# A hybrid decoder layer with a mixture of experts on one core: down weights issued first on the DMA queue, row lists copied at the top of a block, activations turned at its end

## The chip, the cores and the metric

The kernel runs on one core of a Trainium2 chip. The metric is device time in microseconds (us) of one launch; the profile takes one execution and gives its span, which is a little shorter than the time.

## What is computed

One layer of a conditioned decoder for 1024 prompt tokens and 8 sample tokens, width 1024. A mixer part (adaLN, one wide input projection, a gated linear recurrence beside a short convolution, an output projection) is followed by a mixture of experts: 64 experts of width 256, 8 for each token. The experts' part, cut to what matters:

```python
def swiglu(x, w_gate, w_up, w_down):
    return (jax.nn.silu(x @ w_gate) * (x @ w_up)) @ w_down
# assignments sorted by expert, each expert's rows padded to blocks of 128 rows
def block(args):
    tok, e = args
    return swiglu(h_pad[tok], w_gate[e], w_up[e], w_down[e])
out = lax.map(block, (row_tok.reshape(n_blocks, MOE_BLOCK), blk_exp))
out = out.reshape(n_rows, D) * row_w[:, None]
return jax.ops.segment_sum(out, row_tok, num_segments=T + 1)[:T]
```

All inputs and outputs are f32. The change touches only this part.

## The kernel before, in words

The first 1090 us or so hold the mixer, the router and the sorting of rows. Then the function `experts` runs one body (`block_of(i, q)`) for each used block of 128 rows, 92 here, on every engine at once: a Fori over spans of 8 blocks, an If that skips an empty span, a Fori over two parts of 4 blocks, and 4 blocks unrolled, each under an If (`blocks`, L1937 to L1945). Each If loads a number from the tensor `table` into a register (`entry`, L1934), and further `entry` calls fetch a block's expert. These loads, branches and register operations are done by the engine's sequencer, which hands the arithmetic to the engine. Five engines share the work of a block:

- **POOL** gathers the 128 token rows of block i+4 (`gather`, L2050) and adds the result of block i to `acc_d` in HBM (L2070); each addition waits until the one before has landed.
- **PE** turns the gathered rows (`turn`, L2090, 8 transposes), multiplies by gate and up weights (`up`, L2099, 24 matmuls; each product is made of three with operands split into a rounded part `_hi` and a rest `_lo`), turns the gated activations `hh` (L2114, 2 transposes into bank 3) and multiplies by the down weights (6 matmuls at L2124 for the first half of the 256 rows, 4 at L2130, in f32, for the second). Its body for block i has the order: turn `hh` of block i, turn the rows of block i+2, `up` of block i+1, down of block i.
- **ACT** rounds: the turned rows (`take`, x_hi), the weights (`round_weights`, wexp_hi, two halves, and `round_down`, down_hi, between them), the turned activations (hTe is `h1`, L2183; hTe_hi is `h0_hi`, L2184). It also makes the silu (`gate`, sg, L2170), and the output rows `ob` scaled by the routing weight (L2192).
- **DVE** makes the rests: wexp_lo (L2214), down_lo (L2220), x_lo (L2204), hTe_lo (`turned`, L2224); the product sg times up (`gate`, L2228, which gives semaphore `h_ok`); and copies one column of `lists` for the gather (`to_gather`, L2231) and for the addition (`to_add`, L2234), and the routing weights (wcol, L2210), for which it waits for the gathered rows.
- **SP** issues the weight loads of an expert into one of four slots: gate and up, 2 MB in four transfers (`next_up`, L1882), once DVE has made the rests of the expert four before; down, 1 MB in two (`next_down`, L1895), once the down load before has landed and the expert four before has been used. Its loop takes, for expert n: gate and up of n, wait that those of n-1 have landed (`landed_up`), down of n-3.

Of the kernel before, what the change touches and what calls it, by code (L numbers as in the profile page):

```python
# [1898 lines left out]
def experts(nc, tidy, a, sb, sem, banks, ident, xe_d, acc_d, table, starts, total, lists, ix, xg, gat, wexp, wdn, up_in, down_in,  # L1899
# [3 lines left out]
    with ExitStack() as ctx:  # L1903
# [60 lines left out]
        with nc.Block() as block:  # L1964
            @block.sync
            def _(sp):
                def blocks_to(e):

                    return sp.value_load(starts[0:1, bass.ds(e, 1)], min_val=1, max_val=ITEMS)

                def landed_up(slot, round_):
                    sp.wait_ge(up_in[slot], 64 * round_ + 64)
                    sp.sem_inc(up_ok, 1)

                def next_up(part, g):

                    at, slot = part * EG + g, g % RING
                    sp.wait_ge(wlo_ok, blocks_to(at - 3) * 2)
                    load_up(sp, a, wexp, expert_at(part, g), slot, up_in[slot])

                def next_down(part, g):

                    at, slot = part * EG + g, g % RING
                    before = blocks_to(at - 3)
                    sp.wait_ge(down_in, 32 * at)
                    sp.wait_ge(dn_ps, before)
                    sp.wait_ge(dlo_ok, before)
                    load_down(sp, a, wdn, expert_at(part, g), slot, down_in)

                landed_up(0, 0)  # L1990
                landed_up(1, 0)
                for e in range(2, RING):
                    load_up(sp, a, wexp, expert_at(0, e), e, up_in[e])
                    sp.wait_ge(down_in, 32 * e)
                    load_down(sp, a, wdn, expert_at(0, e), e, down_in)
                for e in range(2, RING):
                    landed_up(e, 0)
                for j in range(RING, EG):
                    next_up(0, j)
                    if j > RING:  # L2000
                        landed_up(j - 1 - RING, 1)
                next_down(0, RING)
                with sp.Fori(1, GRP) as part:
                    for g in range(EG):
                        next_up(part, g)
                        if g in (0, RING):
                            landed_up(RING - 1, part * 2 - 1 + g // RING)
                        else:
                            landed_up((g - 1) % RING, part * 2 + g // RING)
                        next_down(part - (0 if g >= 3 else 1), (g - 3) % EG)  # L2010
                landed_up(RING - 1, E // RING - 1)
                for g in range(EG - 3, EG):
                    next_down(GRP - 1, g)
                for slot in range(2):
                    sp.wait_ge(wlo_ok, blocks_to(E - 3 + slot) * 2)
                    for t in range(4 * slot, 4 * slot + 4):
                        sp.dma_start(kept_tile(wexp, t), x2_d[t * P:(t + 1) * P, :]).then_inc(kept_in, 16)
                sp.wait_ge(wlo_ok, blocks_to(E - 1) * 2)
                sp.dma_start(kept_tile(wexp, TILES - 1)[0:NS, :], x2_d[T:, :]).then_inc(kept_in, 16)
                sp.dma_start(kept_tile(wexp, TILES), mod_d[NS:NS + 1, 5 * D:].to_broadcast([P, D])).then_inc(kept_in, 16)  # L2020
                sp.dma_start(kept_tile(wexp, TILES + 1)[0:NS, :], mod_d[0:NS, 5 * D:]).then_inc(kept_in, 16)
                sp.dma_start(kept_tile(wexp, TILES + 2), a["final_norm_g"].rearrange("(a n) -> a n", a=1).to_broadcast([P, D])
                             ).then_inc(kept_in, 16)
                sp.wait_ge(down_in, 32 * E)
                sp.wait_ge(kept_in, 16 * (TILES + 3))
                n = blocks_done(sp)
                sp.wait_ge(wlo_ok, n * 2 + 5)
                sp.sem_inc(ended, 1)
                sp.wait_ge(gu_ps, n + 1)
                sp.sem_inc(ended, 1)  # L2030
                sp.wait_ge(dn_ps, n)
                sp.sem_inc(ended, 1)
                sp.wait_ge(added[0], ((n + 1) >> 1) * 16 + 16)
                sp.sem_inc(passed, 1)
                sp.wait_ge(added[1], (n >> 1) * 16 + 16)
                sp.sem_inc(ended, 1)
                last.sync(sp)
# [46 lines left out]
            def _(pe):  # L2084
# [9 lines left out]
                def up(j, b):  # L2094
# [6 lines left out]
                                             stop=(k == KD - 1 and n == 2))  # L2101
                    last.then_inc(gu_ps, 1)

                pe.sem_inc(ob_ok, 2)
                turn(0, 0, 16)
                turn(1, 1, 16)
                up(0, 0)

                def block_of(i, q):
                    b = q % 2  # L2110
                    e = entry(pe, i, 1, E - 1)
                    pe.wait_ge(h_ok, i + 1)
                    for f in range(FF // P):
                        last = pe.transpose(banks[3][:, f * P:(f + 1) * P], hh[:].rearrange("p (n f) -> p f n", f=FF // P)[:, f, :], ident[:])  # L2114
                    last.then_inc(h_tp, 1)
                    turn(i + 2, (q + 2) % RING, gathered(i, q, 2))
                    up(i + 1, 1 - b)
                    slot = e & (RING - 1)
                    pe.wait_ge(ob_ok, 2 * i + 2)
                    pe.wait_ge(h0lo_ok, i + 1)  # L2120
                    pe.wait_ge(dlo_ok, i + 1)
                    for half in range(2):
                        for n, (stat, mov) in enumerate(((h0_hi, d0_hi), (h0_hi, d0_lo), (h0_lo, d0_hi))):
                            last = pe.matmul(banks[4 + half][:], stat[:], mov[:, half * 512:half * 512 + 512], start=(n == 0),  # L2124
                                             stop=False)
                    last.then_inc(d0_ps, 1)
                    pe.wait_ge(h1_ok, i + 1)
                    pe.wait_ge(down_in, e * 32 + 32)
                    for half in range(2):
                        last = pe.matmul(banks[4 + half][:], h1[:],  # L2130
                                         wdn[:, bass.ds(slot, 1), 1, half * 512:half * 512 + 512].rearrange("p a n -> p (a n)"),
                                         start=False, stop=True)
                    last.then_inc(dn_ps, 1)

                blocks(pe, block_of)
                n = blocks_done(pe)
                pe.wait_ge(wlo_ok, n * 2 + 5)
                pe.wait_ge(ob_ok, n * 2 + 2)
                pe.wait_ge(kept_in, 16 * (TILES + 3))
                last.tensor(pe)  # L2140
# [2 lines left out]
            def _(act):  # L2143
# [24 lines left out]
                def gate(j):  # L2168
                    act.wait_ge(gu_ps, j + 1)
                    act.activation(sg[:], banks[0][:, 0:FF], ACT.Silu).then_inc(sg_ok, 1)  # L2170

                take(0, 0)
                round_weights(0, 0)
                take(1, 1)
                round_weights(1, 1)
                round_down(0)
                gate(0)
                round_weights(2, 0)

                def block_of(i, q):  # L2180
                    b = q % 2
                    act.wait_ge(h_tp, i + 1)
                    act.activation(h1[:], banks[3][:, P:FF], ACT.Copy).then_inc(h1_ok, 1)  # L2183
                    act.activation(h0_hi[:], banks[3][:, 0:P], ACT.Copy).then_inc(h0hi_ok, 1)  # L2184
                    take(i + 2, b)
                    gate(i + 1)
                    round_weights(i + 3, 1 - b, lambda: round_down(i + 1))
                    act.wait_ge(dn_ps, i + 1)
                    act.wait_ge(wc_ok, i + 1)
                    act.wait_ge(ixs_ok, i + 1)  # L2190
# [8 lines left out]
            def _(dve):  # L2199
# [26 lines left out]
                def gate(j):  # L2226
                    dve.wait_ge(sg_ok, j + 1)
                    dve.tensor_tensor(hh[:], sg[:], banks[0][:, FF:], ALU.mult).then_inc(h_ok, 1)  # L2228
# [16 lines left out]
                    rest_of_weights(e, 1, 1, g)  # L2245
                rest_of_down(entry(dve, 0, 1, E - 1), 0)
                gate(0)
                e = entry(dve, 2, 1, E - 1)
                weight(e, 2, 16)
                rest_of_weights(e, 2, 0, 0)  # L2250

                def block_of(i, q):
                    b = q % 2
                    rest_of_weights(entry(dve, i + 2, 1, E - 1), i + 2, b, 1)
                    turned(i)
                    take(i + 2, b)
                    to_gather(i + AHEAD, (q + AHEAD) % RING)
                    gate(i + 1)
                    dve.wait_ge(added[b], (i - b) * 8 + 16)
                    dve.sem_inc(passed, 1)  # L2260
# [2 lines left out]
                    weight(e, (q + 3) % RING, gathered(i, q, 3))  # L2263
                    rest_of_weights(e, i + 3, 1 - b, 0)
                    rest_of_down(entry(dve, i + 1, 1, E - 1), i + 1)

                dve.wait_ge(added[0], 16)
                dve.wait_ge(added[1], 16)
# [152 lines left out]
```

## Time and profile before

| | |
|---|---|
| time, median of 3 runs | 2053.75 us (2050.73 to 2054.92) |
| time of the profiled execution | 2051.39 us |
| its span | 2049.8 us |
| PE busy in the span | 1904.5 us (93%) |
| DVE, ACT, POOL busy | 1158.3 us (57%), 968.6 us (47%), 389.9 us (19%) |
| mean bandwidth over the span | 195 GB/s |

An engine's busy time counts its arithmetic alone. A name such as DVEq or PEldq is the engine's sequencer: its register operations, loads and branches are shown in rows of their own. "issue" as a releaser means that the profile names no other engine or transfer for which the engine had waited. Times within the span count from its start.

### The profile page before, as it was taken

To read this page: it belongs to the slowest core of one execution; us is meant where nothing else is said; L and a number is where in the kernel's file an instruction comes from. 1 tells how busy PE (TensorE), PEld (TensorE's weight loads), DVE (VectorE), ACT (ScalarE), POOL (GpSimd) and SP (SyncE) were. 2 spreads that over 40 slices of the span, in tenths; PEclk is the share of its full clock that TensorE was granted. 3 is DMA by queue.
4 is the path that set the end of the run, shared out by engine and by line. 5 is a ranking of instruction groups with operands and counts; after the bars stand their busy time and mean duration, and the time that the engine had idled before them with its cause. 6 is when DMAs were issued, how large, how long until landed. Compare 5 with 4: busy or idle time off the path is not lost. (4 is left out here: it accounts for less than half of the span.)

```text
span 2049.8 us, 37459 instructions
## 1 busy us (share of the span) xinstructions
PE 1904.5 (93%) x10449; PEld 1527.3 (75%) x10450; DVE 1158.3 (57%) x1715; ACT 968.6 (47%) x1395; POOL 389.9 (19%) x335
## 2 busy tenths in 40 slices
PE   4999999899899999989789999999999999999995
PEld 3999999899788666755547776777777777777772
DVE  4113401166438335545427777777677777778775
ACT  5110111244212222221247777777777777777773
POOL 0100100111111000000203323232233223223330
PEclk9999999999899999999889999999999999999998
DMA  7211311111443665425069896998998889898964
GB/s 260 74 51 42 122 53 31 32 63 62 145 139 115 229 230 205 143 85 196 1 231 312 253 345 174 326 315 283 329 297 285 263 268 319 232 347 260 314 193 176
DMA packets 181813, 399.63 MB, mean 195 GB/s; under 512 B 22137, under 2 KB 86897, under 8 KB 181758
## 3 DMA queue, kind: packets, MB, share of 16 engines
q1 hardware_dynamic: 149166, 312.16, 42.7%
q0 software_dynamic: 31392, 82.49, 15.6%
q10 hardware_dynamic: 1200, 4.26, 0.6%
q8 instruction: 33, 0.54, 0.1%
q14 instruction: 22, 0.18, 0.0%
HBM read 350.16 MB, written 80.64 MB: 210 GB/s over the span
## 5 line engine op out<-in xcount | busy, mean ns | idle before, releaser
L2214 DVE TENSOR_TENSOR wexp_lo<-wexp,wexp_hi 128x2048 fp32r<-128x2048 f32 x189 | 432.6, 2290 | 101.3 <-ACT wexp_hi L2156 65.5
L2156 ACT ACTIVATE wexp_hi<-wexp 128x2048 fp32r x190 | 362.2, 1908 | 44.6 <-issue 42.6
L2099 PE MATMUL bank<-wexp_hi,x_hi 128*128 128x512 f32 x744 | 300.2, 403 | 3.8 <-DVE wexp_lo L2214 3.8
L2099 PE MATMUL bank<-wexp_hi,x_lo 128*128 128x512 f32 x744 | 291.9, 392 | 0.0
L2099 PE MATMUL bank<-wexp_lo,x_hi 128*128 128x512 f32 x744 | 290.6, 391 | 0.0
L2070 POOL DMA_INDIRECT acc_d<-ob,ixs x92 | 171.0, 1859 | 573.3 <-DMA acc_d<-ob,ixs 302.6
L548 PE MATMUL bank<-hT_hi,w_hi 128*128 128x344 f32 x576 | 187.5, 326 | 7.3 <-DVEq L660 7.3
L548 PE MATMUL bank<-hT_hi,w_lo 128*128 128x344 f32 x576 | 185.3, 322 | 0.0
L548 PE MATMUL bank<-hT_lo,w_hi 128*128 128x344 f32 x576 | 184.8, 321 | 0.0
L2130 PE MATMUL bank<-wexp_down,hTe 128*128 x368 | 173.5, 593 | 0.0
L2099 PEld LDWEIGHTS bank<-wexp_hi,x_lo 128*128 128x128 f32 x744 | 140.3, 189 | 31.1
L2099 PEld LDWEIGHTS bank<-wexp_hi,x_hi 128*128 128x128 f32 x744 | 140.5, 189 | 30.2 <-issue 4.2
L2099 PEld LDWEIGHTS bank<-wexp_lo,x_hi 128*128 128x128 f32 x744 | 140.8, 189 | 27.1
L711 PE MATMUL bank<-hT_hi,wg_hi 128*128 128x344 f32 x384 | 129.5, 337 | 12.8 <-POOLq L118 6.7
L634 DVE TENSOR_TENSOR w_lo<-w_raw,w_hi 128x1024 fp32r<-128x1024 f32 x27 | 33.1, 1225 | 186.7 <-POOL w_hi L538 170.4
L2050 POOL DMA_INDIRECT xg<-xe_d,ix x94 | 112.0, 1191 | 91.4 <-DVE ixs L2234 40.9
L711 PE MATMUL bank<-hT_lo,wg_hi 128*128 128x344 f32 x384 | 124.7, 325 | 0.0
L711 PE MATMUL bank<-hT_hi,wg_lo 128*128 128x344 f32 x384 | 124.7, 325 | 0.0
L2204 DVE TENSOR_TENSOR x_lo<-bank,x_hi 128x512 fp32r<-128x512 f32 x188 | 120.1, 680 | 0.6 <-ACT x_hi L2147 0.6
L2220 DVE TENSOR_TENSOR down_lo<-wexp_down,down_hi 128x1024 fp32r<-128x1024 f32 x93 | 113.4, 1219 | 12.5 <-ACT down_hi L2166 12.5
L2170 ACT ACTIVATE sg<-bank 128x256 f32<-128x256 f32 x93 | 35.9, 386 | 168.0 <-PE bank L2099 148.2
L548 PEld LDWEIGHTS bank<-hT_hi,w_hi 128*128 128x128 f32 x576 | 108.9, 189 | 7.6 <-DVEq L660 7.6
(369 smaller groups left out, 3446.2 us busy)
## 6 DMA issues: line engine op xcount, KB each, us to landing
wexp<-in_w_exp_gate SPq DMA_DIRECT2D x128, 512.0 KB
wexp<-in_w_exp_up SPq DMA_DIRECT2D x128, 512.0 KB
wexp_down<-in_w_exp_down SPq DMA_DIRECT2D x128, 512.0 KB
wada<-in_w_ada SPq DMA_DIRECT2D x12, 2048.0 KB, 10.7
w_raw<-in_w_in SPq DMA_DIRECT2D x44, 512.0 KB, 3.9
gates_d<-gst POOLq DMA_DIRECT2D x48, 172.0 KB, 2.1
gate<-gates_d SPq DMA_DIRECT2D x16, 516.0 KB, 5.6
xn<-in_x_prompt ACTq DMA_DIRECT2D x8, 512.0 KB, 8.4
```

The lines of the kernel that those rows point to most:

```text
L548: last = pe.matmul(bank, stat(k), mov(k), start=(k == 0 and x == 0), stop=(k == KD - 1 and x == 2))
L634: dve.tensor_tensor(w_lo[c // 2][:, c % 2], raw[:], w_hi[c // 2][:, c % 2], ALU.subtract).then_inc(w_ready, 1)
L711: last = pe.matmul(banks[7][:, 0:PIECE], stat[j][:, k, :], mov[:, k, toks], start=(k == 0 and x == 0), stop=(k == KD - 1 and x == 2))
L2050: pool.indirect_dma_start(out=xg[:, q % ROOMS, 0:XW], out_offset=None, in_=xe_d, in_offset=bass.IndirectOffsetOnAxis(ap=ix[q][:, 0:1], axi ...
L2070: pool.indirect_dma_start(out=acc_d, out_offset=bass.IndirectOffsetOnAxis(ap=ixs[b][:, 0:1], axis=0), in_=ob[:, b, :], in_offset=None, bou ...
L2099: last = pe.matmul(banks[0][:].rearrange("p (g n) -> p g n", g=2), stat[:, b, k, :], mov[:, b, :, k * FF:(k + 1) * FF], start=(k == 0 and ...
L2130: last = pe.matmul(banks[4 + half][:], h1[:], wdn[:, bass.ds(slot, 1), 1, half * 512:half * 512 + 512].rearrange("p a n -> p (a n)"), star ...
L2156: act.activation(w_hi[:, b, g, :], wexp[:, bass.ds(e & (RING - 1), 1), g, :].rearrange("p a n -> p (a n)"), ACT.Copy).then_inc(whi_ok, 1)
L2170: act.activation(sg[:], banks[0][:, 0:FF], ACT.Silu).then_inc(sg_ok, 1)
L2204: dve.tensor_tensor(x_lo[:, b, at, :].rearrange("p k n -> p (k n)"), banks[1 + half][:], x_hi[:, b, at, :].rearrange("p k n -> p (k n)"), ...
L2214: dve.tensor_tensor(w_lo[:, b, g, :], wexp[:, bass.ds(e & (RING - 1), 1), g, :].rearrange("p a n -> p (a n)"), w_hi[:, b, g, :], ALU.subtr ...
L2220: dve.tensor_tensor(d0_lo[:], down_first(e), d0_hi[:], ALU.subtract).then_inc(dlo_ok, 1)
```

## The change

Four things move; nothing is computed differently.

1. SP's loop issues down of n-3 ahead of gate and up of n, instead of behind them and behind the wait for n-1.
2. DVE copies the row list of the gather at the top of its body.
3. The two transposes of `hh` for block i+1 stand at the end of PE's body for block i, behind the down matmuls, instead of at the start of the body for block i+1. The loop's and the Ifs' loads and branches lie between the two places.
4. ACT rounds the turned activations of block i+1 at the end of its body for block i, ahead of the output rows `ob` of block i, with one more wait (`dn_ps`, since bank 3 and the h tiles are read by the down matmuls). DVE makes their rest at the end of its body too, ahead of the loop's and the If's loads.

```diff
@@ SP: @@
                     for g in range(EG):
+                        next_down(part - (0 if g >= 3 else 1), (g - 3) % EG)
                         next_up(part, g)
                         if g in (0, RING):
                             landed_up(RING - 1, part * 2 - 1 + g // RING)
                         else:
                             landed_up((g - 1) % RING, part * 2 + g // RING)
-                        next_down(part - (0 if g >= 3 else 1), (g - 3) % EG)
@@ PE: @@
+                def turn_rows(j):
+                    pe.wait_ge(h_ok, j + 1)
+                    for f in range(FF // P):
+                        last = pe.transpose(banks[3][:, f * P:(f + 1) * P], hh[:].rearrange("p (n f) -> p f n", f=FF // P)[:, f, :], ident[:])
+                    last.then_inc(h_tp, 1)
...
                 up(0, 0)
+                turn_rows(0)
                 def block_of(i, q):
                     b = q % 2
                     e = entry(pe, i, 1, E - 1)
-                    pe.wait_ge(h_ok, i + 1)
-                    for f in range(FF // P):
-                        last = pe.transpose(banks[3][:, f * P:(f + 1) * P], hh[:].rearrange("p (n f) -> p f n", f=FF // P)[:, f, :], ident[:])
-                    last.then_inc(h_tp, 1)
                     turn(i + 2, (q + 2) % RING, gathered(i, q, 2))
                     up(i + 1, 1 - b)
...
                     last.then_inc(dn_ps, 1)
+                    turn_rows(i + 1)
...
                 pe.wait_ge(wlo_ok, n * 2 + 5)
+                pe.wait_ge(h0lo_ok, n + 1)
@@ ACT: @@
+                def turned(j):
+                    act.wait_ge(h_tp, j + 1)
+                    if j is not 0:
+                        act.wait_ge(dn_ps, j)
+                    act.activation(h1[:], banks[3][:, P:FF], ACT.Copy).then_inc(h1_ok, 1)
+                    act.activation(h0_hi[:], banks[3][:, 0:P], ACT.Copy).then_inc(h0hi_ok, 1)
...
                 gate(0)
+                turned(0)
                 round_weights(2, 0)
                 def block_of(i, q):
                     b = q % 2
-                    act.wait_ge(h_tp, i + 1)
-                    act.activation(h1[:], banks[3][:, P:FF], ACT.Copy).then_inc(h1_ok, 1)
-                    act.activation(h0_hi[:], banks[3][:, 0:P], ACT.Copy).then_inc(h0hi_ok, 1)
                     take(i + 2, b)
                     gate(i + 1)
                     round_weights(i + 3, 1 - b, lambda: round_down(i + 1))
+                    turned(i + 1)
                     act.wait_ge(dn_ps, i + 1)
@@ DVE: @@
                 gate(0)
+                turned(0)
...
                 def block_of(i, q):
                     b = q % 2
+                    to_gather(i + AHEAD, (q + AHEAD) % RING)
                     rest_of_weights(entry(dve, i + 2, 1, E - 1), i + 2, b, 1)
-                    turned(i)
                     take(i + 2, b)
-                    to_gather(i + AHEAD, (q + AHEAD) % RING)
                     gate(i + 1)
...
                     rest_of_down(entry(dve, i + 1, 1, E - 1), i + 1)
+                    turned(i + 1)
```

How it moves instructions is seen at two places. The first is PE, at the seam between two blocks within a part: the difference of the two orders, where L2112 and L2114 of before are the transposes of `hh` (L2107 of after), L2130 and L2133 the last down matmul, L1944 and L1934 the If and its load, and L2086 the first register operation of `turn`. (The two pieces are the end of one body and the start of the next.)

```order
-L2130 MATMUL bank<-wexp_down,hTe 128x512
...
+L2133 MATMUL bank<-wexp_down,hTe 128x512
+L2107 MATMUL bank<-ident,sg 128x128 x2
 L1944 UNCONDITIONAL_BRANCH
 L1934 ISA
...
 L1934 ISA x2
-L2112 REGISTER_ALU
-L2114 MATMUL bank<-ident,sg 128x128 x2
 L2086 ISA
```

The transposes, and with them the wait for `h_ok`, have gone from behind the seam's loads and branches to ahead of them.

The second is DVE at the same seam. Before, from the rest of the down weights to the turned activations' rest (`hTe_lo`):

```order
L2220 TENSOR_TENSOR down_lo<-wexp_down,down_hi 128x1024
L1944 UNCONDITIONAL_BRANCH
L1934 ISA
L1934 TENSOR_LOAD table
L1934 ISA x2
L1944 COMPARE_AND_BRANCH
L1934 ISA
L1934 TENSOR_LOAD table
L1934 ISA x2
L2213 ISA
...
L2214 TENSOR_TENSOR wexp_lo<-wexp,wexp_hi 128x2048
...
L2224 TENSOR_TENSOR hTe_lo<-bank,hTe_hi 128x128
```

And in the changed kernel, from the same operation on:

```order
L2231 TENSOR_TENSOR down_lo<-wexp_down,down_hi 128x1024
L2235 TENSOR_TENSOR hTe_lo<-bank,hTe_hi 128x128
L1944 UNCONDITIONAL_BRANCH
L1934 ISA
L1934 TENSOR_LOAD table
L1934 ISA x2
L1944 COMPARE_AND_BRANCH
L2242 ISA
L2242 COPY ix<-lists 128x1
L1934 ISA
L1934 TENSOR_LOAD table
...
L2225 TENSOR_TENSOR wexp_lo<-wexp,wexp_hi 128x2048
```

The rest `hTe_lo`, which waits for ACT's `h0_hi`, now stands ahead of the seam's loads and of the second half of wexp_lo.

## Rows read from the trace of the kernel before

**Rows 1.** The page: busy time of each engine (share of the span).
```profile
PE 1904.5 (93%) x10449; PEld 1527.3 (75%) x10450; DVE 1158.3 (57%) x1715; ACT 968.6 (47%) x1395; POOL 389.9 (19%) x335
```
**Rows 2.** Chain of waits, 1621 to 1642 us: start us, us, what.
```profile
1629.81 0.23 PE bank L2114 x2
1630.04 0.87 PE bank L2090 x8
1630.91 5.48 PE bank L2099 x24
1636.39 1.36 PE bank L2124 x6
1637.76 1.72 PE bank L2130 x4
```
**Rows 3.** Timeline of PE: start us, us; the first matmul of the same `up`.
```profile
1630.67 0.47 PE L2099 MATMUL bank<-wexp_hi,x_hi 128*128 128x512 f32 x1
```
**Rows 4.** L2124 from 1100 to 2010 us: ns min/median/max, first and last start.
```profile
L2124 PE MATMUL bank<-down_hi,hTe_lo x180: 387/389/628, 1103.4 to 1997.1; 128*128 128x512 f32 x180
```
**Rows 5.** Waits of PE's weight loads, 1100 to 2010 us: total us, times, longest.
```profile
PEld bank L2114 <- issue: 54.0, 163, 2.5
PEld bank L2124 <- issue: 20.4, 24, 3.1
```
**Rows 6.** Waits, 1200 to 1950 us, ACT's for down weights.
```profile
ACT down_hi L2166 <- DMA wexp_down<-in_w_exp_down: 25.3, 11, 4.6
```
**Rows 7.** ACT from 1630 us on, timeline: start us, us, what.
```profile
1630.42 1.90 ACT L2156 ACTIVATE wexp_hi<-wexp 128x2048 fp32r x1
1632.23 1.25 ACT L2192 ACTIVATE ob<-bank,wcol 128x512 f32<-128x512 f32 x2
1633.37 0.27 ACT L2183 ACTIVATE hTe<-bank 128x128 f32<-128x128 f32 x1
1633.52 0.28 ACT L2184 ACTIVATE hTe_hi<-bank 128x128 fp32r<-128x128 f32 x1
```
**Rows 8.** DVE from 1627 us on, timeline.
```profile
1627.19 0.42 DVE L2228 TENSOR_TENSOR sg<-sg,bank 128x256 f32<-128x256 f32 x1
...
1633.14 2.28 DVE L2214 TENSOR_TENSOR wexp_lo<-wexp,wexp_hi 128x2048 fp32r<-128x2048 f32 x1
1635.35 0.28 DVE L2224 TENSOR_TENSOR hTe_lo<-bank,hTe_hi 128x128 fp32r<-128x128 f32 x1
1635.55 1.28 DVE L2204 TENSOR_TENSOR x_lo<-bank,x_hi 128x512 fp32r<-128x512 f32 x2
```
**Rows 9.** DVE's sequencer around `turned`, lines L2223 and L2203, 1632 to 1634.5 us.
```profile
L2223 DVEq ALU_OP  x1: 45/45/45, 1632.8 to 1632.8; - x1
L2203 DVEq ALU_OP  x1: 40/40/40, 1633.9 to 1633.9; - x1
```
**Rows 10.** PE's sequencer around L2114, and the gate on DVE, 1092 to 1095 us.
```profile
L2112 PEldq ALU_OP  x1: 36/36/36, 1093.3 to 1093.3; - x1
L2228 DVE TENSOR_TENSOR sg<-sg,bank x1: 422/422/422, 1093.9 to 1093.9; 128x256 f32<-128x256 f32 x1
L2086 PEldq FUSED_REGOPS  x1: 42/42/42, 1094.4 to 1094.4; - x1
```
**Rows 11.** PE's sequencer from L2130 to L2086: within a part (1548), between spans (1636).
```profile
L2130 PEldq FUSED_REGOPS  x2: 56/58/60, 1548.4 to 1548.5; - x2
L2086 PEldq FUSED_REGOPS  x1: 42/42/42, 1550.4 to 1550.4; - x1
L2130 PEldq FUSED_REGOPS  x2: 56/58/60, 1636.0 to 1636.1; - x2
L2086 PEldq FUSED_REGOPS  x1: 47/47/47, 1640.3 to 1640.3; - x1
```
**Rows 12.** DVE's sequencer from L2220 to L2213, within a part.
```profile
L2220 DVEq FUSED_REGOPS  x1: 57/57/57, 1630.7 to 1630.7; - x1
L2213 DVEq FUSED_REGOPS  x1: 53/53/53, 1632.5 to 1632.5; - x1
```

## The prediction

> **What bounds the kernel now.** The page comes first: PE is busy for 93% of the span and DVE for 57% [rows 1], so PE is the engine to follow. The chain of waits over two calm blocks then holds PE alone: `up` 5.48, first down matmuls 1.36, second ones 1.72, the two transposes of `hh` 0.23, the eight of `turn` 0.87 [rows 2]. These add to 9.66 us, the least time of a block. Third, what blocks really take: L2124 comes twice a block, 180 times, so 90 blocks lie between its first start at 1103.4 and its last at 1997.1 [rows 4]. Less the one step within the last block (0.68, half of 1.36), that is 893.0 us over 89 steps, 10.03 us each. So 0.37 x 89 = 33 us of the experts' part are PE's stalls, and the change can give back no more.
>
> The waits of PE's weight loads say where they stand. Ahead of L2114 there are 54.0 us in 163 waits [rows 5]. A calm block has gaps of some 0.24 us here that cost nothing (the matmul before is still running), and 163 of those are 39 us; so about 11 to 15 us are real. They stand where a span of eight blocks ends: PE's sequencer needs 4.2 us from the last down matmul handed over to the first instruction of `turn` there, against 1.9 within a part [rows 11]. Ahead of L2124 there are 20.4 us in 24 waits [rows 5]. ACT waits 25.3 us, 11 times, for down weights [rows 6]; then `down_hi`, `down_lo` and the down matmuls come late. I put 13 of the 20.4 us to late down weights and the rest to a late DVE. Some 5 us of late gathers and start-up remain of the 33.
>
> **The change, part by part.**
>
> *Down weights first.* No transfer is added. A down load is issued one expert earlier and no longer stands behind 2 MB of gate and up weights. A block's 9.66 us or more is what this gains in lead; the longest wait was 4.6 us [rows 6]. So I count the 13 us as gone (bounds: nothing, and all of the 20.4). Gate and up weights then land later by the 1 MB put ahead; they are loaded almost four experts ahead, and this lead covers it.
>
> *Row list copied at the top.* The copy of one column is only moved. The gather may start up to some 2 us sooner. Gathers cost PE little now, so I count 1 us.
>
> *Activations turned ahead of the seam.* Here it matters whether a sequencer goes on while an instruction it has handed over still waits for its semaphore. The rows say no. On DVE, the register operation ahead of `turned` ran at 1632.8, and the next one, L2203, only at 1633.9 [rows 9]; ACT's `h0_hi`, for which `turned` waits, ended at 1633.52 + 0.28 = 1633.8 [rows 7]. `turned` itself executed at 1635.35 [rows 8], so the engine was not what held the sequencer. On PE, L2112 ran at 1093.3 and the next operation at 1094.4, right behind the end of the gate, 1093.9 + 0.42 [rows 10]. Before the change both waits stand behind the seam's loads. Now they stand ahead of them, and those loads can't run beforehand.
>
> The chain that results covers two blocks. I work it out from the block whose `up` starts at 1621.01, a calm 9.66 before the 1630.67 of the next [rows 3].
> - ACT's second half of wexp_hi starts at 1630.42, and what follows it on ACT at 1632.23 [rows 7]. In the changed kernel this is h1, then `h0_hi` 0.15 later, which lasts 0.28: 1632.66.
> - DVE's sequencer is released 0.05 later and needs the seam: 1.8 from L2220 to L2213 [rows 12], less 0.13 of handing over, plus 0.1 for the list copy and 0.3 to start (estimates from the same rows). wexp_lo starts at 1634.7, where it started at 1633.14 [rows 8].
> - x_lo follows 2.2 later (as 1635.35 follows 1633.14), the gate at x_lo's end, 1.2 to 1.3 after that (x_lo lasts 1.28), and lasts 0.42 [rows 8]: its end is 1638.5.
> - PE's sequencer is released 0.05 later and needs its seam, 1.9 [rows 11]: `turn` starts at 1640.4. It takes 0.87 [rows 2]: the `up` two blocks on starts at 1641.3.
>
> Two blocks take 20.3 us, not 19.3: 10.13 a block. **Cost: 0.47 x 91 = 43 us.**
>
> *Seams between parts and spans.* PE's seam is 2.3 longer at the end of a span [rows 11], and I take 0.6 more between parts (an estimate). Both now lie in the chain: about 2.8 for eight blocks, 11 times, 31 us. Now 11 of these are paid. **Cost: 20 us**; 13 if the release alone counts (stall = seam less the 2.2 us between the gate's end, 6.6 us into a block, and `turn`, 8.8 into it: some 24 in all, less 11).
>
> *Late DVE.* `turned` is ready long ahead of L2124, so the other waits there and the gathers' vanish under the longer block: 5 us gained. *ob* starts 0.3 us later, since two short operations go ahead; in the loop a longer block hides this, at the end it costs 0.3.
>
> **Sum:** 43 + 20 - 13 - 5 - 1 = +44 us on the profiled execution's own 2051.39, its span being 2049.8: 2095.4. That execution was 2.4 us faster than the median of the runs shown, so I forecast 2097 against 2053.75.
>
> **The rivals.**
>
> *A: the waits don't hold the sequencers.* Then both engines run their seams while the gate is still out, and the stalls of spans (11), late down weights (13) and late DVE (some 3) go: 27 us faster, 2027. For it speaks only that each seam's work is then nearly all under cover. Against it stand [rows 9] and [rows 10]; it decides at one place, whether the register operation behind `hTe_lo` runs before or after `h0_hi` ends. The Trainium skill states this rule (Perfetto Trace Analysis, section Per-engine timelines, for DVE, ACT and the tensor engine): an instruction goes into a wait queue and its sequencer is then ready for the next. By that rule the change would gain its 27 us. The trace disagrees, by 1.1 us of waiting on DVE [rows 9] and 1.1 on PE [rows 10].
>
> *B: only PE's wait counts.* If DVE finds slack that I don't see (it is busy for 57%), the gate ends as now at 1627.61, 6.6 us into the block [rows 8]; with 1.9 for the seam `turn` starts at 8.5, under its present 8.8 (9.66 less 0.87, [rows 2]). Calm blocks then cost nothing, seams 13, and 13 + 5 are gained: about 2049 to 2054. Against it: DVE's seam can't start before 1632.7, and wexp_lo, x_lo and the gate behind it are 4 us of work in a row.
>
> *C: the down weights stay late*, because the transfers themselves are what is short. Then the 13 us are not gained: 2110. Against it: a longer block leaves more time to each load.
>
> **How the numbers follow.** My forecast has 0.80, A 0.09, B 0.06, C 0.05. Within the forecast, the chain may be off by 0.15 us a block (14 us), and the seams by 7. The range goes from 2072 to 2116: it holds C and most of the forecast, and leaves out A and B. Faster by over 0.2% (about what a measurement of this kernel can tell from no change, 4 us): A and a third of B, 0.11. Slower by over 0.2%: 0.85. Within: 0.04.
>
> **What would show it.** In the profile after: DVE idles about 1 us ahead of the second half of wexp_lo (L2225, behind the list copy), which starts 1.5 us later in the block than now. The gate on DVE ends 7.6 or more into a block, where it ended at 6.6. PE's waits move from L2114 and L2124 to `turn`, and add to some 80 us or more; every second block is longer than 10.5 us and the ones between near 9.7. ACT's waits for down weights are gone. If PE waits ahead of `turn` only at the ends of spans, B is right; if L2235's successor on DVE's sequencer runs ahead of `h0_hi`'s end, A.

## The result, and the profile after

The changed kernel takes **2130.99 us** (median of 4 runs, 2123.79 to 2134.5) against 2052.24 for the kernel before on the same chip (median of 4, 2050.24 to 2054.92): a ratio of 1.0378, 95% interval 1.0356 to 1.0401, or 79 us slower. The forecast was 44 slower, with a range that ended at 2116. So the direction and, as will be seen, the chain were right, and the size was not. The profiled execution took 2129.97 us.

The page, its lines on the span and on busy time, to be held against [rows 1]:

```profile
span 2128.4 us, 37283 instructions
PE 1924.3 (90%) x10451; PEld 1547.8 (73%) x10452; DVE 1167.3 (55%) x1716; ACT 969.4 (46%) x1397; POOL 432.4 (20%) x335
...
L2070 POOL DMA_INDIRECT acc_d<-ob,ixs x92 | 222.7, 2420 | 643.0 <-DMA acc_d<-ob,ixs 366.0
L2099 PE MATMUL bank<-wexp_hi,x_hi 128*128 128x512 f32 x744 | 306.5, 412 | 3.8 <-DVE wexp_lo L2225 3.8
```

The span grew by 78.6 us. PE's busy time grew too, by 19.8 us, though it has the same matmuls to do: something makes its instructions longer. The mean of this group of `up` (L2099) is 412 ns; before it was 403. That is the clock, to which I come below.

**The experts' part.** The down matmuls of the 90 blocks between 1100 us and the end, counterpart of [rows 4] (L2124 is now L2127):

```profile
L2127 PE MATMUL bank<-down_hi,hTe_lo x180: 389/389/389, 1107.3 to 2074.1; 128*128 128x512 f32 x180
```

(2074.1 - 1107.3 - 0.7) / 89 = 10.86 us a block, where it was 10.03: 73 of the 79 us lie here. Of the rest, about 4 lie in the first three blocks (the fourth `up` starts at 1101.3 instead of 1097.4; the first starts at 1065.6 instead of 1065.8) and 2 behind the last.

**The chain of waits, 1847 to 1893 us**: start us, us, what. It covers the end of a span and two calm blocks, and answers to [rows 2].

```profile
1848.79 5.49 PE bank L2099 x24
1854.28 1.36 PE bank L2127 x6
1855.64 1.72 PE bank L2133 x4
1857.35 0.23 PE bank L2107 x2
1857.58 2.62 issue
1860.20 1.96 PE bank L2090 x8
1862.16 6.22 PE bank L2099 x24
...
1871.45 0.23 PE bank L2107 x2
1871.68 0.87 PE bank L2090 x8
1872.55 5.49 PE bank L2099 x24
...
1881.11 0.23 PE bank L2107 x2
1881.34 0.73 issue
1882.07 1.09 PE bank L2090 x8
1883.16 5.47 PE bank L2099 x24
...
1891.94 0.87 PE bank L2090 x8
```

Read it from below. The calm pair: the two blocks from 1872.55 to 1892.81 take 20.3 us, 10.6 and 9.65, and all of the loss is one "issue" of 0.73 (with a first transpose that is 0.2 longer) ahead of `turn` (L2090) in every second block. The forecast said 20.3 us for two blocks. The end of the span: 2.62 us of "issue", and then something that was in no term of the sum: `turn` takes 1.96 instead of 0.87 and `up` 6.22 instead of 5.49.

**DVE and ACT in the same block**, timelines; the block's `up` starts at 1872.31 in the timeline, first row (the chain gives it 0.2 later, behind its weight load), and all places in the block are counted from there. They answer to [rows 3], [rows 7] and [rows 8].

```profile
1872.31 0.47 PE L2099 MATMUL bank<-wexp_hi,x_hi 128*128 128x512 f32 x1
```

```profile
1872.07 1.91 ACT L2161 ACTIVATE wexp_hi<-wexp 128x2048 fp32r x1
1873.87 0.26 ACT L2181 ACTIVATE hTe<-bank 128x128 f32<-128x128 f32 x1
1874.03 0.27 ACT L2182 ACTIVATE hTe_hi<-bank 128x128 fp32r<-128x128 f32 x1
```
```profile
1874.79 0.28 DVE L2235 TENSOR_TENSOR hTe_lo<-bank,hTe_hi 128x128 fp32r<-128x128 f32 x1
1875.26 0.15 DVE L2242 COPY ix<-lists 128x1 uint32 x1 [0.19 <-issue]
1876.33 2.29 DVE L2225 TENSOR_TENSOR wexp_lo<-wexp,wexp_hi 128x2048 fp32r<-128x2048 f32 x1 [0.91 <-issue]
1878.54 1.28 DVE L2215 TENSOR_TENSOR x_lo<-bank,x_hi 128x512 fp32r<-128x512 f32 x2
1879.74 0.41 DVE L2239 TENSOR_TENSOR sg<-sg,bank 128x256 f32<-128x256 f32 x1
```

The second half of wexp_lo starts 4.0 us into the block (it was 2.5), because DVE's sequencer waited for `h0_hi` ahead of its seam. The seam's first register operation runs as soon as `h0_hi` has ended at 1874.03 + 0.27 = 1874.3, half a microsecond before `hTe_lo` itself gets its turn on the engine (1874.79). Sequencer of DVE, L1934, 1873 to 1876.3 us:

```profile
L1934 DVEq FUSED_REGOPS  x4: 82/138/190, 1874.3 to 1875.7; - x4
L1934 DVEq TENSOR_LOAD <-table x2: 303/303/303, 1874.5 to 1875.4; - x2
```

The gate ends at 1880.15, 7.84 us into the block (6.6 before; the forecast said 7.6 or more). PE's seam begins right behind it, at 1880.2, and `turn` starts at 1882.07, 1.9 us behind the gate's end. That is the forecast's chain, link by link. Sequencer of PE, L1934 and L2086, 1879.3 to 1882.2 us:

```profile
L1934 PEldq FUSED_REGOPS  x4: 46/106/151, 1880.2 to 1881.6; - x4
L2086 PEldq FUSED_REGOPS  x1: 42/42/42, 1881.9 to 1881.9; - x1
```

**Waits from 1100 to 2090 us** (total us, times, longest), which answer to [rows 5]:

```profile
PEld bank L2090 <- issue: 87.9, 53, 3.8
DVE wexp_lo L2225 <- issue: 83.6, 104, 0.9
PE bank L2090 <- issue: 74.8, 48, 3.6
PEld bank L2107 <- issue: 38.2, 162, 0.2
```

PE's waits have moved to `turn`, as forecast, and are 88 us where some 80 or more were foretold. The waits ahead of L2107 are the 0.24 us gaps that cost nothing. ACT no longer waits for down weights between 1200 and 1950 us.

**TensorE's clock.** Windows of the changed kernel: us, PE busy (instructions) and the other engines, granted clock, DMA share, GB/s. The second stretch is the one behind the long wait above.

```profile
1848.55:1860.10 11.55, 9.03 (x39) 6.68 (x37) 9.58 (x12) 9.36 (x14) 4.13 (x2) 1.00 1.02 338
1860.20:1863.60 3.40, 3.40 (x12) 3.08 (x13) 0.91 (x3) 2.22 (x4) 0.00 (x0) 0.50 1.03 311
```

The granted clock is 1.00 (2.4 GHz) up to the wait and 0.50 (1.2 GHz) for the 3.4 us that follow 2.6 us in which PE stood idle. The changed kernel has some 41 us at 0.50 in the blocks of the experts' part, in ten pieces: seven at PE's wait at the end of a span, three behind one at the end of a part. The kernel before has one piece of 3.4 us. Over longer stretches (PE alone), first of the changed kernel, then of the kernel before:

```profile
1500.00:1800.00 300.00, 274.52 (x1214) 0.98 0.81 262
1800.00:1990.00 190.00, 173.94 (x770) 0.98 0.84 266
```
```profile
1500.00:1800.00 300.00, 296.13 (x1335) 1.00 0.87 279
1800.00:1990.00 190.00, 185.11 (x837) 1.00 0.89 287
```

### The profile page after: what moved, and what is told of

Same layout as the page of the kernel before. It is cut to its first block, busy times and chain, and to the rows that moved or that the text cites. A ratio compares the mean times of both kernels' runs of the same rounds, so it can differ in the third digit from the quotient of the medians.

```text
span 2128.4 us, 37283 instructions
## 1 busy us (share of the span) xinstructions
PE 1924.3 (90%) x10451; PEld 1547.8 (73%) x10452; DVE 1167.3 (55%) x1716; ACT 969.4 (46%) x1397; POOL 432.4 (20%) x335
## 4 chain that ended last, share of the span: by engine, by line
PE 40%; issue 5%; DMA 3%; DVE 1%; ACT 1%; ACTq 0%; POOLq 0%; DVEq 0%; POOL 0%
PE bank L2099 22%; PE bank L2133 6%; PE bank L2127 5%; PE bank L2090 4%; DMA acc_d<-ob,ixs 2%; DMA xg<-xe_d,ix 2%; PE bank L2107 1%; PE bank L2336 1%; DVE yy L2398 0%; ACTq L1934 0%; ACT ob L2203 0%; POOLq L1934 0%; DVE wexp_lo L2225 0%; PE bank L2341 0%; DVE aa L2379 0%
## 5 line engine op out<-in xcount | busy, mean ns | idle before, releaser
L2070 POOL DMA_INDIRECT acc_d<-ob,ixs x92 | 222.7, 2420 | 643.0 <-DMA acc_d<-ob,ixs 366.0
L2099 PE MATMUL bank<-wexp_hi,x_hi 128*128 128x512 f32 x744 | 306.5, 412 | 3.8 <-DVE wexp_lo L2225 3.8
L2099 PE MATMUL bank<-wexp_hi,x_lo 128*128 128x512 f32 x744 | 296.3, 398 | 0.0
L2099 PE MATMUL bank<-wexp_lo,x_hi 128*128 128x512 f32 x744 | 296.2, 398 | 0.0
L2090 PE MATMUL bank<-ident,xg 128*128 128x128 f32 x752 | 108.0, 290 | 86.2 <-issue 77.8
L2133 PE MATMUL bank<-wexp_down,hTe 128*128 x368 | 172.7, 591 | 0.0
L2099 PEld LDWEIGHTS bank<-wexp_hi,x_hi 128*128 128x128 f32 x744 | 144.7, 195 | 31.7 <-issue 4.2
L2099 PEld LDWEIGHTS bank<-wexp_hi,x_lo 128*128 128x128 f32 x744 | 143.5, 193 | 31.9
L2099 PEld LDWEIGHTS bank<-wexp_lo,x_hi 128*128 128x128 f32 x744 | 144.8, 195 | 28.0
L2090 PEld LDWEIGHTS bank<-ident,xg 128*128 128x128 f32 x752 | 87.5, 148 | 97.7 <-issue 97.3
L2203 ACT ACTIVATE ob<-bank,wcol 128x512 f32<-128x512 f32 x184 | 116.6, 693 | 0.0
## 6 DMA issues: line engine op xcount, KB each, us to landing
wada<-in_w_ada SPq DMA_DIRECT2D x12, 2048.0 KB, 10.6
```

Source lines behind the costliest of these rows:

```text
L2070: pool.indirect_dma_start(out=acc_d, out_offset=bass.IndirectOffsetOnAxis(ap=ixs[b][:, 0:1], axis=0), in_=ob[:, b, :], in_offset=None, bou ...
L2090: last = pe.transpose(banks[1 + k // 4][:, (k % 4) * P:(k % 4 + 1) * P], xg[:, q % ROOMS, k * P:(k + 1) * P], ident[:])
L2099: last = pe.matmul(banks[0][:].rearrange("p (g n) -> p g n", g=2), stat[:, b, k, :], mov[:, b, :, k * FF:(k + 1) * FF], start=(k == 0 and ...
L2133: last = pe.matmul(banks[4 + half][:], h1[:], wdn[:, bass.ds(slot, 1), 1, half * 512:half * 512 + 512].rearrange("p a n -> p (a n)"), star ...
L2203: act.activation(ob[:, b, 512 * half:512 * half + 512], banks[4 + half][:], ACT.Copy, scale=wcol[:, q:q + 1]).then_inc(ob_ok, 1)
```

## The experiments

My theory, M below: waits hold the sequencers, so each wait that was moved ahead of a seam puts the seam into a chain gate, PE's seam, `turn`, DVE's seam, wexp_lo, x_lo, gate; what the sum lacked is the low clock behind the longer idle times. The runs were taken in three sets, each with the kernel before beside it (2050.66 to 2051.55 us); differences between runs are taken from the ratios.

### The parts of the change one by one

```diff
                     for g in range(EG):
+                        next_down(part - (0 if g >= 3 else 1), (g - 3) % EG)
                         next_up(part, g)
...
-                        next_down(part - (0 if g >= 3 else 1), (g - 3) % EG)
```

> Only SP's order is changed, against the kernel before. Theory M (the cost of the change is the activations' move; the down weights first are a gain): the 13 us of late down weights go, 2039 to 2042 us against 2052, ACT's 25.3 us of waits ahead of down_hi fall below 3, PE's wait ahead of the first down matmuls falls from 20.4 to some 7. Rival S (the new order on SP delays gate and up weights and so carries part of the slowdown): 2060 or more, with waits for weights ahead of wexp_hi.

Measured: 2043.09 us, ratio 0.9952 (0.9935 to 0.9969), 10 us faster. Waits from 1200 to 1950 us: none of ACT's for down weights is left, and PE's ahead of the first down matmuls, 19.9 us in 23 before in this stretch, are

```profile
PEld bank L2124 <- issue: 9.1, 21, 1.4
```

M holds, though the time is 1 us above my range: my 13 us were 3 too many, and are just inside the interval.

The changed kernel with SP's order and the list copy as they were (the diff above reversed, and `to_gather` back behind `take`):

> The changed kernel with SP's order and the list copy as before, so only the activations' move is left. Theory M: all of the slowdown is here: 2131 us if the longer blocks hide the late down weights anyway, up to 2144 if they don't. Rival S (a good part of the slowdown comes from SP's order): 2110 or less.

Measured: 2124.54 us, ratio 1.0361 (1.0335 to 1.0388). The whole slowdown is in the activations' move: the interval overlaps that of the full change, and the time is 6 below the 2131 that I expected. So beside the move, SP's new order gains nothing: ACT waits only once for down weights in this run (1.2 us), since a longer block hides them anyway. S falls.

The list copy alone, in the kernel before:

```diff
                     b = q % 2
+                    to_gather(i + AHEAD, (q + AHEAD) % RING)
                     rest_of_weights(entry(dve, i + 2, 1, E - 1), i + 2, b, 1)
                     turned(i)
                     take(i + 2, b)
-                    to_gather(i + AHEAD, (q + AHEAD) % RING)
```

> Only the list copy at the top of DVE's body, against the kernel before. Theory M: the gather starts 2 us sooner, of which PE needs little: 2050 to 2053 against 2052. Rival L (the copy at the top delays the second half of wexp_lo and so the gate): 2055 or more.

Measured: 2051.03 us, ratio 1.0004 (0.9993 to 1.0015): nothing either way.

### One wait behind its seam again

DVE's `turned` goes back to its old place; PE and ACT stay as changed.

```diff
                     rest_of_weights(entry(dve, i + 2, 1, E - 1), i + 2, b, 1)
+                    turned(i)
                     take(i + 2, b)
...
                     rest_of_down(entry(dve, i + 1, 1, E - 1), i + 1)
-                    turned(i + 1)
```

> The changed kernel, but DVE makes hTe_lo again behind its seam, after the second half of wexp_lo; PE and ACT stay as changed, so only PE's sequencer waits ahead of its seam. Theory M: calm blocks go back to 9.66 us, stalls stay at the ends of spans (some 13 us, and some us of lower clock behind them), the down weights' 13 us are gained: 2050 to 2065. Rival P (PE's wait is what costs most, DVE's hides): 2100 or more.

Measured: 2071.68 us, ratio 1.0104 (1.0083 to 1.0126): 21 us slower than before, and 56 faster than the whole change. The calm blocks are 9.66 us again and the gate ends 6.60 into the block. Waits, 1100 to 2090 us:

```profile
PEld bank L2090 <- issue: 37.7, 33, 2.6
DVE wexp_lo L2225 <- issue: 18.0, 43, 1.0
```

P falls. I expected 2050 to 2065 and was low by 7. What lies above it: `turn` waits in the first block of each part as well as of each span (10.2 and 11.9 us against 9.66), and 17 us of the blocks are at the low clock, by my estimate up to 8 us of loss (half of it, since work takes twice as long there).

Now the other way round: PE's transposes of `hh` go back to the head of the block, behind PE's seam; DVE and ACT stay as changed.

```diff
                     e = entry(pe, i, 1, E - 1)
+                    turn_rows(i)
                     turn(i + 2, (q + 2) % RING, gathered(i, q, 2))
...
                     last.then_inc(dn_ps, 1)
-                    turn_rows(i + 1)
```

> The changed kernel, but PE's two transposes of hh stand at the head of the block again, behind its seam; DVE and ACT stay as changed. Theory M: the gate still ends at some 7.8 us into every second block (DVE waits ahead of its seam), but PE takes it up only at 8.6, so calm blocks are 9.66 us again and no stall or low clock of TensorE is added: 2040 to 2050 us. Rival D (DVE's wait costs time by itself): 2080 or more, blocks of 10 us or longer.

Measured: 2062.19 us, ratio 1.0052 (1.0034 to 1.007), 11 us slower than before and 67 faster than the whole change. The mechanism is M's: the gate ends 7.8 to 8.0 us into most calm blocks, and these are still 9.66 us, for PE takes it up only at 8.63 (the weight load of its transposes). But the time is 12 above what I expected. PE is no longer late at a span's end, and so DVE's own long seam there comes into the open. DVE, timeline, at a span's end, in a block whose `up` starts at 1643.44:

```profile
1645.91 0.28 DVE L2235 TENSOR_TENSOR hTe_lo<-bank,hTe_hi 128x128 fp32r<-128x128 f32 x1
1648.08 0.15 DVE L2242 COPY ix<-lists 128x1 uint32 x1 [1.89 <-issue]
1649.17 2.29 DVE L2225 TENSOR_TENSOR wexp_lo<-wexp,wexp_hi 128x2048 fp32r<-128x2048 f32 x1 [0.94 <-issue]
...
1652.58 0.41 DVE L2239 TENSOR_TENSOR sg<-sg,bank 128x256 f32<-128x256 f32 x1
```

The gate ends 9.55 us into the block, and the block takes 10.74. A later DVE also copies the routing weights and the row lists later, and gathers come late: the block behind this one has a median of 10.4 us. Waits, 1100 to 2010 us:

```profile
PE bank L2090 <- DMA xg<-xe_d,ix: 22.6, 23, 2.7
```

Both runs hold SP's new order, which alone is worth 10 us. Against that run (0.9952) DVE's wait alone costs 20 us, PE's alone 31, and the two together 87. They meet in one chain, in which DVE's seam makes the gate late, and PE's seam comes behind the gate. A part of the excess is the clock: 7 and 17 us of the blocks are at 0.50 with one wait, 41 with both. ACT's move stays in both runs, so it has no price of its own here.

### The clock

Two matmuls that nobody waits for, behind the transposes of `hh` of every fourth block:

```diff
                     turn_rows(i + 1)
+                    if q == RING - 1:
+                        for f in range(2):
+                            pe.matmul(banks[6][:], ident[:], ident[:].unsqueeze(1).to_broadcast([P, 4, P]), start=True, stop=True)
```

> The changed kernel plus two f32 matmuls of 512 columns (some 0.86 us each) into an unused bank, behind the transposes of hh of every fourth block, so that PE works where it stood idle ahead of a part's or a span's seam; nothing waits for them. Theory M with the clock: TensorE's granted clock stays at its upper level in the experts' part, where the changed kernel has some 41 us at 0.50, and 15 to 22 us come back: 2109 to 2116 us. Rival K (the drops have nothing to do with PE's idle time, or cost nothing): 2131 us or more.

Measured: 2116.54 us, ratio 1.0315 (1.0295 to 1.0334): 13 us less than the changed kernel, for more work, and the two intervals don't overlap. The granted clock is 1.00 in all the blocks (columns as above, PE alone):

```profile
1200.00:1500.00 300.00, 287.97 (x1274) 1.00 0.85 279
1500.00:1800.00 300.00, 285.00 (x1257) 1.00 0.81 262
1800.00:1990.00 190.00, 182.55 (x804) 1.00 0.84 275
```

The blocks that stood behind a span's end, 10.4 us on average in the changed kernel, are 9.65 now; the 89 blocks lose 14.3 us in sum. The gain is 2 below my range. Half of the 41 us would be 20; that part of what the slow matmuls lose would have been waited for in the next seam anyway is my explanation, and was not tried. K falls: the low clock follows PE's idle time, and costs.

### The seams

Spans of 16 blocks instead of 8 (`SPAN = 16`), in the changed kernel and in the kernel before:

> The changed kernel with spans of 16 blocks instead of 8, so six of the eleven ends of a span become ends of a part. Theory M: each of the six gives back 1.8 us of seam (13.3 against 11.5 us for the block in the trace of the changed kernel) and about half of the time at low clock: 13 to 20 us less, 2111 to 2118 us. Rival N (the long blocks there come from something else that recurs every eight blocks, the weights of SP's loop say): 2128 us or more.

> The kernel before with spans of 16 blocks. Theory M: the span's seam is nearly under cover here (10.4 us a block against 9.66), so six fewer give back 4 to 8 us: 2043 to 2048 us. Rival N: no difference, 2050 us or more.

Measured: 2119.58 us, ratio 1.0312 (1.0284 to 1.034), 14 less than the changed kernel (my range of 2111 to 2118 ended 2 us lower); and 2045.71, ratio 0.9975 (0.9962 to 0.9989), 5 less than before. Both gains are as M has it: the same places are worth two to three times as much where the seam stands in the chain (their loss of clock included).

Then the seams between the four blocks of a part, taken out:

```diff
-                        for q in range(RING):
-                            i = span * SPAN + part * RING + q
-                            with eng.If(entry(eng, i, 0, E) < E):
-                                body(i, q)
-                            eng.nop()
+                        with eng.If(entry(eng, span * SPAN + part * RING, 0, E) < E):
+                            for q in range(RING):
+                                body(span * SPAN + part * RING + q, q)
+                        eng.nop()
```

> The changed kernel with one If around the four blocks of a part instead of one around each (right for these data, whose 92 blocks are 23 full parts; a last part that is not full would go wrong). The loads and branches between the four blocks are gone, those between parts and spans stay. Theory M: with no seam behind a wait, three of four blocks lose nothing by the move; at a part's end DVE's seam and PE's no longer meet in one chain (a late gate is followed by no seam of PE), so what is left is PE's seam of 2.3 us at a span's end and 0.5 at a part's: 2050 to 2065 us. Rival Q (it is the order on ACT, the later output rows or the additions of POOL that cost): 2100 us or more.

> The kernel before with the same single If for a part. Theory M: between the four blocks its seams were under cover, so little is gained: 2042 to 2051 us, and the gap between the two kernels falls from 79 us to 20 or less. Rival Q: the gap stays at 50 or more.

Measured: 2064.15 us, ratio 1.0056 (1.0034 to 1.0078), for the changed order, and 2048.3, ratio 0.9978 (0.9962 to 0.9994), for the old one. The gap between the two orders falls from 79 us to 16, and no arithmetic, addition or gather of PE, ACT, DVE or POOL was changed, nor its order. This is the clearest of the runs: Q falls. The seams go on all four engines at once; that those of DVE and PE count is what the two runs above show. Waits of the changed order with one If, 1100 to 2090 us (`turn` is L2089 there):

```profile
PEld bank L2089 <- issue: 42.6, 33, 2.7
PE bank L2089 <- issue: 26.6, 19, 2.5
PE bank L2089 <- DMA xg<-xe_d,ix: 9.9, 13, 2.1
```

What is left is at the ends of parts (median of the block 10.7 us) and spans (11.6).

### A version that beats both

> A version meant to beat both: the kernel before with SP's new order and spans of 16 blocks. If the two gains measured alone (10 and 5 us) add up: 2034 to 2039 us. If the late down weights and the span's seam hid each other: 2040 to 2044.

> The same with spans of 32 blocks, three ends of a span fewer: 2032 to 2038 us if each is worth 0.8 us as measured; no better than spans of 16 if what is left at these places is the part's end.

Measured: **2038.87** us, ratio 0.9925 (0.9902 to 0.9949), and **2034.81**, ratio 0.9916 (0.9895 to 0.9937). The two gains (10 and 5 us alone) add up, and the version with spans of 32 is 17 us faster than the kernel before; whether 32 is better than 16 these runs can't tell. In the profile with spans of 32 the first block of every eight has a median of 9.66 us, where it was 10.42 in the kernel before.

## Why the prediction was wrong in size

- **That a wait holds its sequencer** (against rival A): right. DVE's seam begins at 1874.3, when `h0_hi` ends, PE's at 1880.2, when the gate has ended, and the one-If runs show what this is worth. Rival A's 2027 us are 104 below what was measured. A holds with the rule of the Trainium skill (Perfetto Trace Analysis, Per-engine timelines) that the sequencer is ready for its next instruction once it has pushed one into the wait queue; the trace of the changed kernel is against it here, by the same two places.
- **Two-block chain, 0.47 us a block**: right. The calm pairs (the third and fourth block of each part) have medians of 10.7 and 9.7 us. Rival B, with PE's wait alone, is close to the run in which DVE's was put back: 2072 instead of 2049 to 2054. So B was priced too low as well; some 8 us of that are its clock, by the estimate above, and the rest was not taken apart.
- **Seams of parts and spans, +20**: the mechanism right, the term too small. In the filler run, which has no low clock, the pairs of blocks with a span's or a part's seam take 22.5 and 21.5 us in the mean, 44.0 together where two pairs of 20.3 and the 2.8 made 43.4; over the eleven spans 7 us are missing.
- **"The other waits there and the gathers' vanish under the longer block: 5 us gained", and 1 for gathers**: this step failed. Calm pairs have a mean of 20.7 us, not 20.3, while their medians add to 20.4: some late blocks remain. In the filler run the 89 blocks take 951.8 us, 15 more than the 893.0 of before and the forecast's 44; less the 7 of the seams, about 8 us are these blocks. What makes them late was not tried.
- **Down weights first, -13**: measured alone, 10. In the changed kernel the late weights are gone with the old order too. The sum stays the same, but the cause is the longer block; rival C had this right in its last sentence, and was no rival.
- **The step that failed by most: TensorE's clock.** The sum put it at nothing, without a reason, though it let PE wait 2 us and more at each end of a span. The filler run puts it at 13 us. The trace of before gave the hint: its one piece at 0.50 in the experts' part, at 1488.4, comes right behind a wait of 2.74 us ahead of L2124, and the waits that came in at the ends of spans are as long (2.62 in the chain above).
- **First blocks and tail**: 6 us (4 in the first three blocks, 2 behind the last) were not counted, but for the 0.3 of *ob*. The last line of the forecast also dropped 0.8 us: 2053.75 and 44 are 2098.

In sum: 44 forecast, 13 clock, 7 seams, 8 late blocks, 6 for both ends: 78 of the 79. Of these the clock is shown by a run that takes it away; the split between seams and late blocks is read from the traces and was not tried by itself. The range was too narrow because it held only errors of the terms I had (14 for the chain, 7 for the seams), and all that was missing lay on the same side.

## What to carry to other kernels

Before a wait is moved, list what stands between its old and its new place on that engine's sequencer, loads, branches and loop ends included: work behind a wait is no longer under cover, however short it looks in busy time. A second such wait on another engine is not priced by itself; look whether the two lie in one chain, where one makes the other's producer late. And when TensorE, hardly ever idle before, gets waits of 2 us or more, price what they do to its clock, too.

## What was unexpected

The granted clock fell to 0.50 again and again around waits of 2.1 to 3.6 us, in a kernel that keeps PE busy for 90% of its span; and two matmuls of no use in every fourth block, 46 in all, made the kernel 13 us faster. Not every such wait went with a drop: of the eleven ends of a span, with waits of 2.6 to 3.6 us, four had none. Between 1944 and 1947 us PE waited 2.8 us, and the clock stayed at 1.00, while waits of 2.1 to 2.2 us at the ends of three parts were followed by a drop. What decides that is open.

The additions of POOL (L2070) take 2420 ns in the mean against 1859, and about as long with the move alone (2413), but 1986 with one If and 1727 with the down weights first. In the chain that ended last they hold 1.6% of the span against 1.9% before, so they don't carry the slowdown; why they take longer, and whether they have a share in the late blocks, was not tried.
